# Feed-forward pairs of an encoder kernel: gate scaling ahead of the fourth weight sum, Silu and the next copy ahead of the late casts, the activation tile written in two steps

## What is computed

```python
def swiglu(xn, w_in, w_out):          # D_MODEL 1024, FF 2816
    gu = xn @ w_in
    g = gu[..., :FF]
    u = gu[..., FF:]
    return (jax.nn.silu(g) * u) @ w_out

...
        xn = rmsnorm(h, norm_ffn[i])
        h = h + swiglu(xn, ffn_w_in[i], ffn_w_out[i])
```

## Time and profile before

| | |
|---|---|
| median of 3 runs | 2041.63 us (2041.41 to 2042.32) |
| the profiled execution | 2041.35 us, its span 2039.5 us |
| mean granted TensorE clock over the span | 0.987 |
| TensorE busy | 97% of the span |
| DVE, POOL, ACT busy | 55%, 53%, 34% |

### The profile page before, as it was taken

The page is one execution under the profiler, slowest core; times in us unless marked ns, Lnnn a source line. Parts: engine busy times, 40 slices in busy tenths (PEclk is TensorE's granted clock), DMA queues, the critical chain, the costliest instruction groups (busy, mean ns, idle before and its releaser), DMA issues.

```text
span 2039.5 us, 30031 instructions
## 1 busy us (share of the span) xinstructions
PE 1981.4 (97%) x11025; PEld 1822.8 (89%) x11025; DVE 1113.2 (55%) x1832; ACT 701.2 (34%) x1393; POOL 1076.9 (53%) x1503
## 2 busy tenths in 40 slices
PE   7999999999999999999999999999898999999998
PEld 7788878799999999999988888887798899998997
DVE  6554453577456255265565666666585472562651
ACT  3322322235143043043324444445353240340431
POOL 4322323257588486596632222221466794884973
PEclk9999999999999999999999999999899999999999
DMA  4111101021122222122211111110121212222213
GB/s 121 42 31 33 41 21 52 21 67 58 45 85 66 60 67 63 57 83 62 71 42 32 32 31 31 31 31 21 42 67 42 83 57 73 75 63 65 73 58 93
DMA packets 215109, 111.59 MB, mean 55 GB/s; under 512 B 6947, under 2 KB 213958, under 8 KB 214998
## 3 DMA queue, kind: packets, MB, share of 16 engines
q1 hardware_dynamic: 210928, 108.29, 18.2%
q10 hardware_dynamic: 4070, 1.81, 0.4%
HBM read 106.93 MB, written 3.15 MB: 54 GB/s over the span
## 4 chain that ended last, share of the span: by engine, by line
PE 89%; DVE 5%; ACT 2%; POOL 2%; issue 1%; DMA 1%; SPq 0%; DVEq 0%; ACTq 0%
PE ps L541 46%; PE ps L606 28%; PE ps L748 4%; PE ps L896 3%; PE ps L864 2%; POOL wl L497 1%; PE ps L732 1%; PE ps L886 1%; PE ps L798 1%; DVE gt L1229 1%; DVE raw L1101 1%; PE ps L757 1%; PE ps L685 0%; DMA wk<-in_x_sample_dram 0%; PE ps L849 0%
## 5 line engine op out<-in xcount | busy, mean ns | idle before, releaser
L486 POOL CAST wh<-raw 128x256 fp32r<-128x256 f32 x432 | 161.7, 414 | 830.6 <-PE ps L541 804.6
L606 PE MATMUL ps<-sx,wh 128*128 128x400 f32 (+1 forms) x1408 | 371.6, 345 | 15.9 <-ACT p L1688 15.9
L497 POOL TENSOR_TENSOR wl<-raw,wh 128x256 fp32r<-128x256 f32 x352 | 311.2, 913 | 87.5 <-ACT wh L1681 87.1
L490 POOL TENSOR_TENSOR wl<-raw,wh 128x256 fp32r<-128x256 f32 x432 | 338.7, 813 | 10.3
L606 PE MATMUL ps<-sx,wxh 128*128 128x400 f32 (+1 forms) x1056 | 275.3, 342 | 5.9 <-DVE ut L1217 3.6
L606 PEld LDWEIGHTS ps<-sx,wh 128*128 128x128 f32 x1408 | 261.1, 191 | 18.7 <-ACT p L1688 18.5
L606 PE MATMUL ps<-sx,wl 128*128 128x400 f32 (+1 forms) x704 | 242.5, 344 | 0.0
L1681 ACT ACTIVATE wh<-raw 128x512 fp32r<-128x512 f32 x176 | 108.1, 628 | 356.0 <-PE ps L541 241.5
L541 PE MATMUL ps<-xh,wh 128*128 128x400 f32 (+2 forms) x768 | 222.8, 368 | 2.7 <-DVE wk L1016 2.6
L497 POOL TENSOR_TENSOR wxl<-raw,wxh 128x256 fp32r<-128x256 f32 x220 | 217.1, 1010 | 14.4 <-ACT wxh L1681 14.3
L541 PE MATMUL ps<-xl,wh 128*128 128x400 f32 (+2 forms) x768 | 212.8, 352 | 0.0
(11 more groups left out here) (234 smaller groups left out, 3214.6 us busy)
## 6 DMA issues: line engine op xcount, KB each, us to landing
raw<-in_ffn_w_in_dram SPq DMA_DIRECT2D x154, 256.0 KB, 3.0
raw<-in_ffn_w_out_dram SPq DMA_DIRECT2D x48, 384.0 KB, 3.2
raw<-in_d_w_in_dram SPq DMA_DIRECT2D x24, 512.0 KB, 3.8
raw<-in_m_w_in_dram SPq DMA_DIRECT2D x22, 512.0 KB, 3.7
rawx<-in_ffn_w_in_dram SPq DMA_DIRECT2D x22, 256.0 KB, 3.1
raw<-in_m_w_out_dram SPq DMA_DIRECT2D x8, 512.0 KB, 3.6
raw<-in_ffn_w_out_dram SPq DMA_DIRECT2D x16, 256.0 KB, 2.8
raw<-in_d_w_out_dram SPq DMA_DIRECT2D x8, 512.0 KB, 3.7
```

The source lines that it names most:

```text
L486: ins = pool.tensor_copy(wh[:, slot, c], raw[:, slot, c])
L490: ins = pool.tensor_tensor(wl[:, slot, c], raw[:, slot, c], wh[:, slot, c].bitcast(F32), ALU.subtract)
L497: ins = pool.tensor_tensor(slot_of(j, 1)[:, c], factor(g, j)[:, c], slot_of(j, 0)[:, c].bitcast(F32), ALU.subtract)
L606: mm = pe.matmul(product_bank(g, j, layer), slot_of(j, low_w)[:, k * P:(k + 1) * P], sx[layer][:, k * NPROD + j, low_x, :], start=(j in OP ...
```

## The change

Nothing is added or taken away on any engine; instructions stand in another order on DVE and ACT, and some waits differ. TensorE, POOL and SP keep their order.

- `gate_scaled(g)` goes ahead of `sum_4(g+1)` where it stood behind it (third pair, first pair of a group) and, at the second pair of a layer, ahead of `sum_3(g+1)`.
- ACT's Silu of these pairs goes ahead of the casts of factors 5 and 6 of the next pair (at the second pair: ahead of `y_high` of the first), and the first copy of the next pair, `product_copy(g+1, 0)`, follows it at once.
- `hidden` ends with the multiplication (line 1196); the low part is a step of its own, `hidden_low`, put behind `sum_1` of the next pair, at the third pair of a layer behind `gate_first_half(g)`, and at the second behind `sum_4`.
- `gate_first_half` waits for the multiplication that read the gate tile, no longer for the low part; `up_second_half` now waits for the low part, which reads the up tile.

```diff
                 def up_second_half(g):
                     ve.wait_ge(prod_done, NPROD * g + 5)
                     ve.wait_ge(copy_ready, 3 * g + 2)
+                    if g > f0 + 1:
+                        ve.wait_ge(yl_ready, y0 + g - f0)
...
                         elif g > f0:
-                            ve.wait_ge(yl_ready, y0 + g - f0)
+                            ve.wait_ge(yt_ready, y0 - D_HEADS * layer + g - f0)
...
-                    split_low(up[:, 0:2 * w], fyh[:, i, 0:2 * w], fyl[:, i, 0:2 * w], y0 + f + 1, yl_ready)
-
-                def finish(g, i):
-                    up_first_half(g)
-                    hidden(g, i)
+
+                def hidden_low(g, i):
+                    up = gate_up(g)[1]
+                    split_low(up[:, 0:2 * w], fyh[:, i, 0:2 * w], fyl[:, i, 0:2 * w], y0 + g - f0 + 1, yl_ready)
...
                             sum_1(g + 1)
                             sum_2(g + 1)
                             gate_second_half(g)
+                            gate_scaled(g)
                             sum_3(g + 1)
-                            hidden(f0, 0)
+                            hidden(f0)
                             sum_4(g + 1)
-                        elif g == f0 + 2 or i == 0:
-                            if i:
-                                finish(g - 1, i - 1)
+                            hidden_low(f0, 0)
+                        elif g == f0 + 2:
+                            up_first_half(g - 1)
+                            hidden(g - 1)
+                            gate_first_half(g)
+                            hidden_low(g - 1, i - 1)
+                            up_second_half(g)
+                            sum_1(g + 1)
+                            sum_2(g + 1)
+                            sum_3(g + 1)
+                            gate_second_half(g)
+                            gate_scaled(g)
+                            sum_4(g + 1)
+                        elif i == 0:
                             sum_1(g + 1)
                             gate_first_half(g)
                             up_second_half(g)
                             sum_2(g + 1)
                             sum_3(g + 1)
                             gate_second_half(g)
+                            gate_scaled(g)
                             sum_4(g + 1)
                         else:
-                            finish(g - 1, i - 1)
+                            up_first_half(g - 1)
+                            hidden(g - 1)
                             if more:
                                 sum_1(g + 1)
+                            hidden_low(g - 1, i - 1)
+                            if more:
                                 sum_2(g + 1)
                                 sum_3(g + 1)
...
-                        gate_scaled(g)
-                    finish(first + tiles - 1, tiles - 1)
+                            gate_scaled(g)
...
                             product_copy(g + 1, 0, layer, p1, C11)
+                            silu(g)
                             y_high(f0, 0)
...
                         if g == f0 + 2:
-                            silu(g - 1)
                             weight_high(g, 6, n0, first)
                             weight_high(g + 1, 0, n0, first)
...
                         else:
-                            product_copy(g, 0, layer, p1, C11)
+                            if i > 1 and g != f0 + 3:
+                                product_copy(g, 0, layer, p1, C11)
...
+                        if i == 0 or g == f0 + 2:
+                            for j in range(2, 5):
+                                weight_high(g + 1, j, n0, first)
+                            silu(g)
+                            product_copy(g + 1, 0, layer, p1, C11)
+                            weight_high(g + 1, 5, n0, first)
+                            weight_high(g + 1, 6, n0, first)
+                            continue
                         if more:
                             for j in range(2, 6):
                                 weight_high(g + 1, j, n0, first)
```

More of the change, by code:

```diff
@@ L1185, in up_first_half, with hidden @@
                                      ALU.mult).then_inc(sum_ready, 1)
-                def hidden(g, i):
-                    f, (gate, up) = g - f0, gate_up(g)
+                def hidden(g):
+                    gate, up = gate_up(g)
                     ve.wait_ge(sum_ready, summed(g, C22))
@@ L1275, in ffn @@
                             gate_second_half(g)
-                        gate_scaled(g)
-                    finish(first + tiles - 1, tiles - 1)
+                            gate_scaled(g)
+                    g = first + tiles
+                    up_first_half(g - 1)
+                    hidden(g - 1)
+                    hidden_low(g - 1, tiles - 1)
                     ends = gi == len(GROUPS) - 1
@@ L1282, in ffn @@
                         continue
-                    g = first + tiles
                     for m in range(KT):
```

## The result

| | before | changed |
|---|---|---|
| median | 2041.63 us (2035.27 to 2043.0, 5 runs) | 2025.52 us (2022.43 to 2026.55, 5 runs) |
| ratio, with its 95% interval | | 0.9923 (0.9906 to 0.9941) |
| span of the profiled execution | 2039.5 us | 2024.7 us |

The change takes 16 us off. A second measurement of both kernels, on the chip of most of the experiments, gave 2026.28 us against 2040.81 (0.9928, 0.9912 to 0.9945), 14.5 us. The executions of the kernel before beside the experiments spread from 2035 to 2043 us, the shortest with a mean granted clock of 0.990 to 0.991 and the longest with 0.987 to 0.988, so that not all of them lose as much to the low clock as the profiled one does.

What follows compares the result with a forecast made beforehand. TensorE, busy 97% of the span, bounds the kernel, so only its waits and low clock could be gained; 6.6 + 11.3 = 17.9 us takes 2041.35 to 2023.4, 2023.7 for the median. Forecast 2021 to 2027, full range 2019 to 2031.

Steps and rivals of the forecast that it cites:

- The meter and the limit: TensorE's weight-load waits in the feed-forward products, 26.7 us, plus 6.3 us of low clock: at most 33 us to gain.
- Part 2: Third and fourth pairs of both layers' first groups: 5.1 us in layer 0, 6.2 in layer 1, together 11.3 us.
- the whole instruction: First groups: by the skill's lock rule the scaling holds POOL 1.0 us, not 0.5; the sum would be 1.0 us smaller.
- Part 1: Six later groups, second pair: `p` waits go, each gains product 6's slack plus 0.3 us, 6.6 us in all.
- the bound of 1.0: Six later groups: `up_second_half` at most 1.0 us earlier, if its wait for POOL shrinks by most of its 1.40.
- the prediction's own sign: Second pair, later groups: waits gone at product 6 would show that POOL was not the bound.
- Layer 1's third group: Layer 1, group 3, where the clock was low: slack 1.65 plus 0.3 at product 6, a gain of 1.9 us.
- the rival of the returning clock: Layer 1's first group: waits of 2.0 and 1.2 us bring back the low clock for 3.1 us, 2027; chance 0.17.
- The first groups' clock: Both layers' first groups: 4.8 us of low clock expected to go, since no wait stays above 2.2 us.
- part 3: Rest of the kernel: late low part and SP's loads cost nothing; POOL's splits and `sum_4` stay within 0.6 us.
- the slower rival: Eight places: split waits at products 4 and 6 cool the clock, 1.7 to 3.1 us each, 2037 to 2049; chance 0.05.
- POOL and DMA: Rival: they hold the six later groups, nothing of the 6.6 us comes, only part 2, 2030.3 us; chance 0.15.

Runs made afterwards that it cites:

- the kernel with the casts ahead: Changed kernel, but ACT casts factors 5 and 6 ahead of Silu and the first copy again, first pair of the six later groups: 2026.73 us, ratio 0.9933.
- part 2 alone: Changed kernel with the six later groups put back to their old order on DVE and ACT, first groups kept changed: 2031.35 us, ratio 0.9952.
- the scaling behind: Changed kernel with the scaling alone put back behind `sum_4`, Silu and copies left as changed: 2037.71 us, ratio 0.9991.

## Why the prediction was right, and where it was not

The forecast was 2023.7 us, measured were 2025.5 and 2026.3: a gain of 16.1 and 14.5 us for 17.9. The two steps were right, the sizes off in places. Point by point:

- **The meter and the limit** (26.7 us of waits, 6.3 of low clock). The waits left are 13.6 us plus 1.4 of clock: 13.1 and 4.9 us came, 18 in all. The meter overstates a little: the groups themselves are 16.4 us shorter. Two readings on the way were off. Product 0 of a pair is ready one product (2.19 us) before product 2 opens, not two; in the changed kernel its copy waits for TensorE until 583.20, 2.2 us after the pair's start. And 71.04 against 69.1 is 1.9, not about 1.5; the 1.5 fits the 1.4 measured for such a stretch. Neither entered a term of the gain.
- **Part 2, 11.3 us.** Measured 4.43 + 5.68 = 10.1. The steps: `sum_4` was not left where it was, it starts 51.66 us after the first product in layer 0 in place of 51.31, and 51.24 in place of 50.92 in layer 1, 0.35 and 0.32 later, since the scaling holds POOL 0.8 us and not 0.5 (four splits 4.10 us in place of 3.27 at layer 0's third pair). The 5.5 us from `sum_4` to product 4 measured 5.53 and 5.42. The three last products take 6.82 and 6.55, not 6.57 and 6.27. That makes 0.63 and 0.52 of the shortfalls of 0.67 and 0.52. The mechanism was right, the term for POOL too small. With the whole instruction, which I had weighed against it, the sum would have been 1.0 us smaller; the `sum_4` part of the shortfall is 0.67.
- **Part 1, 6.6 us.** Measured 3.72 + 2.53 = 6.25. `up_second_half` came 0.66 us earlier, not 0.3, since `sum_3`'s wait for POOL shrank from 1.40 to 0.70 and its own 1.14 to 0.69, which lies within the bound of 1.0 that I had given. Slack 0.72 plus 0.66 would be 1.38 a group in layer 0. Product 6 now waits a little for it: its weight load begins at 594.91, 0.05 us after `up_second_half` ends (594.29 + 0.57), and its first three matmuls take 0.66 us in place of 0.55. The slack counted neither; 1.20 to 1.28 came, against my 1.0:

```profile
594.91 0.30 PEld L606 LDWEIGHTS ps<-sx,wxh 128*128 128x128 f32 x2 [0.21 <-DVE ut L1218]
```

Layer 1's second and fourth group gave 0.94 and 0.95 against 0.85. The waits are shared out otherwise than forecast: product 4 waits 0.6 to 1.0 us in layer 0, not 0.5, and product 6 at most 0.3, not 0.7 to 1.5; in layer 1 product 4 waits 1.6 to 2.1, as forecast. By the prediction's own sign, waits gone at product 6 would mean that POOL is not the bound. That sign misleads: product 4 hides the wait, and with product 4 freed (the copy of `u` ahead) product 6 waits 0.8 to 1.8. That product 4's wait costs nothing of its own holds where product 6 still waits, in four places; in layer 1's third and fourth group it does not wait there, and product 4 alone is the bound. Both are bound within some tenths of a microsecond of each other, which is why the copy of `u` alone brought nothing.
- **Layer 1's third group, 1.9 us.** Measured 0.64. The step that failed: the slack of 1.65 was read from a stretch that the low clock had stretched, so the term counts on full clock there, and the only reason given, for the first groups, is that no wait stays above 2.2 us. This one is 1.82 us by the matmul and 2.1 by the weight load and brought the lower level back for about 1.4 us. It was the rival of the returning clock, at another place than I had put it. That part 1 as a whole came within 0.4 us of its 6.6 is luck in part: this term was 1.3 too large, the five other groups together 0.9 too small.
- **The first groups' clock** did go: 1.00 at 524 and at 1552.
- **Moved to no cost (part 3).** The early Silu and copy count for about a third of part 1, and the low part behind `sum_1`, which I had costed as one reason for the 0.3, turned out to carry it: with it ahead of `sum_1` the kernel is slower than before, by the 0.7 to 0.8 us a group that comes with the scaling's hold on POOL and by the clock. I had not seen this as the slower rival. The order on ACT, the cast of factor 0 ahead of `y_high`, had it in plain sight: once the multiplication is early, that cast waits 1.92 us for its load (in the changed kernel too, at 587.39) and whatever waits for `y_high` waits with it. No run moved the load itself, so what an earlier load would bring stays open.
- **The rivals.** POOL and DMA did not hold the six groups to nothing: they gained 6.25 us, and the time would else have been that of part 2 alone (2030.3 forecast, 2031.35 measured). But what product 4 now waits for is POOL's splits and the load behind them. The split waits did not cool the clock everywhere, only once in eight places.

## What to carry to other kernels

Before a step is moved earlier, follow what it releases down to the next load: where a waiting instruction stands ahead of it in an in-order queue, the gain can turn into a loss, as here, unless the step behind that queue is split off as well. When a wait is freed and time stays, look two products on, since here products 4 and 6 were bound by the same chain of weight sums; only moving every consumer of the bank ahead of that chain freed both, for a further 9 us or so with the fourth pair's copies and the clock in it. And price an instruction that is moved beside another engine's work, from a row if there is one: VectorE's scaling of 0.99 us beside GpSimd's splits cost 0.81, nearly its whole length.

## What the runs showed of the hardware

- A DVE tensor_tensor with both inputs in SBUF of 0.99 us beside POOL's splits makes four of them last 4.09 us in place of 3.28. The other way round, DVE's `sum_3` takes 1.14 us in the midst of POOL's splits and 0.69 where it starts just before POOL's next one (593.20 against 593.31), and `sum_4` makes two splits last 1.89 in place of 1.44.
- The length of a wait alone does not decide the clock. The wait of 1.82 us (matmul's own idle time) before 1757.04 was followed by 0.50, one of 1.74 us before 1616.28 was not, nor the one of 1.99 before 1892.26 with the scaling left out, nor the one of 2.40 before 1613.66 in the kernel with the casts ahead; there, one of 2.23 us at 1754.45 was. Among the later groups it was layer 1's third, and that alone, in the kernel before, the changed one and its repeat, part 2 alone, the scaling behind and the casts ahead; with the low part ahead of `sum_1`, where the waits are 2.4 to 4.1 us, it was four of the six. In the kernels where layer 1's third group waits at most 1.5 us it stayed at 1.00. The Trainium skill ("TensorE: Matmul & The Clock Gate", Part 1) says that the gate's window runs free of the program and does not start anew with the kernel. If so, where a gap falls could count beside its length; these rows agree in so far as length alone does not decide, but a place that recurs in six executions they leave unexplained, and no run was made to tell what marks it. The two stretches of the kernel with the casts ahead:

```profile
1615.00:1617.00 2.00, 2.00 (x13) 1.00 0.48 135
...
1756.00:1758.00 2.00, 2.00 (x8) 0.50 0.40 117
```

- The unchanged code before the first feed-forward product ended between 465.70 and 468.15 us in the profiled executions of these kernels. A difference of 2 us between two spans has to be looked for there first.
